# Last level of a triangular inverse on compact blocks of two matrices, in a two-block transformer kernel

## The reference, cut to what matters

```python
    A = jnp.where(strict, jnp.einsum('bhntk,bhnsk->bhnts', kb, k) * Lmat, 0.0)
    eye = jnp.eye(C, dtype=A.dtype)
    T = lax.linalg.triangular_solve(eye + A, jnp.broadcast_to(eye, A.shape),
                                    left_side=True, lower=True, unit_diagonal=True)
    u = jnp.matmul(T, v * beta[..., None])
    w = jnp.matmul(T, kb * jnp.exp(gam)[..., None])
```

## Time and profile before

| what | value |
|---|---|
| median of 3 runs | 1431.57 us (1431.5 to 1432.8) |
| the profiled execution | 1431.52 us |
| its span, first to last instruction | 1429.8 us |
| TensorE, matmul / weight load | 98% / 93% busy |
| VectorE / ScalarE | 68% / 56% busy |
| mean granted TensorE clock | 0.999 |

### The profile page before, as it was taken

One profiled execution on the slowest core, in us unless ns is written; L12 is line 12 of the kernel. 1 busy time (PEld: TensorE's weight loads), 2 busy tenths in 40 slices (PEclk: granted clock), 3 DMA queues, 4 the chain that ended last, 5 costly groups with the idle time before them and its releaser, 6 DMA issues.

```text
span 1429.8 us, 28104 instructions
## 1 busy us (share of the span) xinstructions
PE 1405.7 (98%) x10598; PEld 1330.5 (93%) x10598; DVE 969.4 (68%) x1441; ACT 799.5 (56%) x1289; POOL 28.7 (2%) x73
## 2 busy tenths in 40 slices
PE   8999999999999999999999999999999999999998
PEld 8999999979999889999899999999999899899997
DVE  5786677676455575555688888888888755654554
ACT  4345444644444454444568788788788743544443
POOL 6000000000000000000000000000000000000000
PEclk9999999999999999999999999999999999999999
DMA  8465555555555645665574444534543356566651
GB/s 257 145 178 147 140 131 156 192 177 177 191 191 176 207 146 177 182 193 183 143 182 119 127 108 117 144 99 112 144 115 119 90 149 206 159 189 186 196 183 59
DMA packets 304641, 224.94 MB, mean 157 GB/s; under 512 B 10419, under 2 KB 288069, under 8 KB 304581
## 3 DMA queue, kind: packets, MB, share of 16 engines
q1 hardware_dynamic: 304580, 224.09, 53.1%
HBM read 223.02 MB, written 1.05 MB: 157 GB/s over the span
## 4 chain that ended last, share of the span: by engine, by line
PE 91%; DVE 4%; ACT 2%; DVEq 1%; issue 1%; POOL 0%; ACTq 0%; POOLq 0%
PE G L1758 19%; PE G L1760 19%; PE G L1759 19%; PE M L1763 5%; PE M L1764 5%; PE M L1765 5%; PE M L1758 2%; PE M L1760 2%; PE M L1759 2%; PE M L2230 1%; DVE w_lo L1045 1%; PE M L2243 1%; PE M L2213 1%; PE M L2202 1%; ACT w_hi L573 1%; DVEq L1042 1%
## 5 line engine op out<-in xcount | busy, mean ns | idle before, releaser
L1758 PE MATMUL G<-xa_hi,w_hi 128*128 128x256 f32 x2152 | 629.4, 292 | 2.0 <-DVE w_lo L1045 1.4
L1045 DVE TENSOR_TENSOR w_lo<-w_raw,w_hi 128x2048 fp32r<-128x2048 f32 (+1 forms) x208 | 475.2, 2286 | 228.7 <-ACT w_hi L573 224.1
L1760 PE MATMUL G<-xa_hi,w_lo 128*128 128x256 f32 x2152 | 608.6, 283 | 0.0
L1759 PE MATMUL G<-xa_lo,w_hi 128*128 128x256 f32 x2152 | 608.2, 283 | 0.0
L573 ACT ACTIVATE w_hi<-w_raw 128x2048 fp32r<-128x2048 f32 x207 | 394.6, 1908 | 236.3 <-PE G L1760 134.2
L1758 PEld LDWEIGHTS G<-xa_hi,w_hi 128*128 128x128 f32 x2152 | 411.0, 191 | 9.4 <-issue 7.1
L1759 PEld LDWEIGHTS G<-xa_lo,w_hi 128*128 128x128 f32 x2152 | 411.2, 191 | 2.8 <-issue 1.7
L1760 PEld LDWEIGHTS G<-xa_hi,w_lo 128*128 128x128 f32 x2152 | 410.5, 191 | 0.1
L1763 PE MATMUL M<-w_hi,xb_hi 128*128 128x512 f32 x304 | 118.9, 391 | 0.9 <-DVE xb_lo L1045 0.7
L1764 PE MATMUL M<-w_lo,xb_hi 128*128 128x512 f32 x304 | 118.7, 390 | 0.0
L1765 PE MATMUL M<-w_hi,xb_lo 128*128 128x512 f32 x304 | 118.3, 389 | 0.0
(11 more groups left out here) (357 smaller groups left out, 2029.3 us busy)
## 6 DMA issues: line engine op xcount, KB each, us to landing
w_raw<-in_w_in SPq DMA_DIRECT2D x166, 512.0 KB, 4.7
w_raw<-in_ffn_w_in SPq DMA_DIRECT2D x88, 512.0 KB, 5.0
w_raw<-in_w_ff SPq DMA_DIRECT2D x64, 512.0 KB, 4.1
w_raw<-in_ffn_w_out SPq DMA_DIRECT2D x44, 512.0 KB, 3.7
w_raw<-in_w_out SPq DMA_DIRECT2D x16, 512.0 KB, 4.2
w_raw<-in_w_branch_gdn SPq DMA_DIRECT2D x16, 512.0 KB, 5.1
w_raw<-in_w_branch SPq DMA_DIRECT2D x12, 512.0 KB, 4.3
w_raw<-in_w_branch_hgrn SPq DMA_DIRECT2D x8, 512.0 KB, 4.0
```

Of the source, the lines that this page charges most:

```text
L1045: return v.tensor_tensor(dst, src, hi.bitcast(F32), ALU.subtract)
L1758: mm(out_, w[0], x[0], start=first, stop=False)
L1759: mm(out_, w[0], x[1], start=False, stop=False)
L1760: return mm(out_, w[1], x[0], start=False, stop=last_)
```

## The change

The last level, too, works on compact blocks. z(6) is two matmul calls with n21 as weights, a new tile that holds the right halves of both matrices of nt; ScalarE fills it at the end of the head before. z_copy(6) and inv_t(5) take the form of the lower levels, so there is a compact(5) on ScalarE. w(6) comes out turned, two calls of 64 columns. yi is then put together from its parts: ScalarE's new `y_diagonal` copies the four diagonal quarters from bank 5 (four instructions of 64 partitions), y_copy(5) copies only the lower right blocks into yc, and VectorE copies w into the off-diagonal quarters with two copies. The tile xc gets space of its own.

In the queues: on ScalarE level_exp(8) moves ahead of the split, and split_j(1) moves behind compact(5) and z_copy(6), ahead of y_copy(5). In the last head ScalarE's split and VectorE's w_low of a later chunk move behind y_diagonal and behind scored(8).

```diff
-    xc = grid(yi.rearrange("p i e c -> p (i e c)")[:, 2 * P:4 * P], i=TT, e=2, c=HD)
+    xc, n21 = (grid(mix(2 * P), i=TT, e=2, c=HD) for _ in range(2))
...
                 act.wait_ge(zz_done, l + (i - 1) * 6)
-                if l == LEVELS - 1:
-                    nc.scalar.activation(halved(zi.rearrange("p i e c -> p (i e c)"), l, 0), packed(M[:, 3, 0:T], l),
-                                         ACT.Copy).then_inc(zc_ready, 1)
-                    return
...
                 else:
-                    nc.scalar.activation(yi.rearrange("p i e c -> p (i e c)"), M[:, 5, :], ACT.Copy).then_inc(yy_ready, 1)
+                    nc.scalar.activation(yc[:, :, HD:P], M[:, 5, 0:T].rearrange("p (i c) -> p i c", i=TT)[:, :, HD:P],
+                                         ACT.Copy).then_inc(yy_ready, 1)
+
+            def y_diagonal():
+                if not main:
+                    return
+                for side in range(2):
+                    half = slice(HD * side, HD * side + HD)
+                    for e in range(2):
+                        ins = nc.scalar.activation(yi[half, :, e, half], M[HD * e:HD * e + HD, 5, 0:T].rearrange(
+                            "p (i c) -> p i c", i=TT)[:, :, half], ACT.Copy)
+                ins.then_inc(yy_ready, 1)
...
             if main:
                 level_exp(7)
-            if gemm:
-                split_j(1)
-            else:
+                level_exp(8)
+            compact(5)
+            z_copy(6)
+            split_j(1)
+            y_copy(5)
+            y_diagonal()
+            if not gemm:
                 act_split(c0 + 5 + RING - 6)
-            if main:
-                level_exp(8)
-            z_copy(6)
-            y_copy(5)
...
                 level_exp(2, i + 1)
+                nc.scalar.activation(n21, nt[:, :, :, HD:P], ACT.Copy)
...
-        v.memset(zi, 0.0)
...
                     dve.wait_ge(wt_done, i)
-                    dve.sem_inc(waited, 1)
-                    v.copy_predicated(halved4(yi, l, 1), halved(lmask[:, l, :].bitcast(I32), l, 1).unsqueeze(1).to_broadcast(shape),
-                                      packed(M[:, 5, 0:T], l).rearrange("p (x n) s -> p x n s", x=4)).then_inc(yy_ready, 1)
+                    for e in range(2):
+                        ins = v.tensor_copy(yi[0:HD, :, e, HD:P],
+                                            M[HD * e:HD * e + HD, 4, 0:P].rearrange("p (i c) -> p i c", i=TT))
+                    ins.then_inc(yy_ready, 1)
...
             decayed(7)
-            if not gemm:
-                w_low(c0 + 5 + RING - 6, i, 6)
             decayed(8)
...
             scored(8)
+            if not gemm:
+                w_low(c0 + 5 + RING - 6, i, 6)
...
                 if l == LEVELS - 1:
-                    four(3, nt, xi, l, 0, zz_done)
+                    for b in range(TT):
+                        ins = mm(M[:, 3, P * b:P * b + P].rearrange("p (e c) -> p e c", e=2), n21[:, b, :, :].rearrange("p e c -> p (e c)"),
+                                 xi[:, b, :, 0:HD], start=True, stop=True)
+                    ins.then_inc(zz_done, 1)
                     return
...
                 if l == LEVELS - 1:
-                    four(5, zi, yi, l, 1, wt_done)
+                    for b in range(TT):
+                        ins = mm(M[:, 4, HD * b:HD * b + HD], zd[:, b, :, :].rearrange("p e c -> p (e c)"), yc[:, b, HD:P],
+                                 start=True, stop=True)
+                    ins.then_inc(wt_done, 1)
                     return
...
-                if l < LEVELS - 2:
-                    pe.wait_ge(xc_ready, l + 1 + (i - 1) * 5)
-                    for b in range(TT):
-                        ins = nc.tensor.transpose(M[:, 5, P * b:P * b + P], xc[:, b, :, :].rearrange("p e c -> p (e c)"), ident[:])
-                    ins.then_inc(yt_done, 1)
-                    return
-                pe.wait_ge(xx_ready, l + (i - 1) * 5)
+                pe.wait_ge(xc_ready, l + 1 + (i - 1) * 6)
                 for b in range(TT):
-                    for e in range(2):
-                        at = T * b + P * e
-                        ins = nc.tensor.transpose(M[:, 5, at:at + P], xi[:, b, e, :], ident[:])
+                    ins = nc.tensor.transpose(M[:, 5, P * b:P * b + P], xc[:, b, :, :].rearrange("p e c -> p (e c)"), ident[:])
                 ins.then_inc(yt_done, 1)
```

More of the change, by code:

```diff
@@ L2207, in level @@
                 ins.then_inc(lev_done, 1)
-            def four(out_bank, lhs, rhs, l, side, done):
-                for b in range(TT):
-                    for e in range(2):
[L2212 to L2215, removed]
             def inv_z(l):
@@ L2237, in inv_w @@
                 pe.wait_ge(zc_ready, l + (i - 1) * 6)
-                pe.wait_ge(yy_ready, l + (i - 1) * 7)
+                pe.wait_ge(yy_ready, l + (i - 1) * 8)
                 if l == LEVELS - 1:
-                    four(5, zi, yi, l, 1, wt_done)
+                    for b in range(TT):
+                        ins = mm(M[:, 4, HD * b:HD * b + HD], zd[:, b, :, :].rearrange("p e c -> p (e c)"), yc[:, b, HD:P],
+                                 start=True, stop=True)
+                    ins.then_inc(wt_done, 1)
                     return
@@ L2282, in head @@
             if main:
-                pe.wait_ge(yy_ready, i * 7)
+                pe.wait_ge(yy_ready, i * 8)
                 for e in range(2):
```

## The result

The changed kernel takes 1438.50 us (median of six runs, 1438.12 to 1439.73), the kernel before 1432.16 us (six runs taken with it, 1431.5 to 1432.8). The ratio is 1.0046, with a 95% interval of [1.0034, 1.0059]: slower by 6.3 us, where 5.3 had been forecast.

What follows compares the result with a forecast made beforehand. TensorE, busy 98%, was taken as the bound, with VectorE having no slack at the border of two heads. 1431.5 + 3.5 (loop) + 1.8 (last head) = 1436.8 us; range 1431.5 to 1440.8 us.

Steps and rivals of the forecast that it cites:

- The loop's term: Borders between heads: each next head begins 0.5 us late, 7 borders x 0.5 = +3.5 us.
- VectorE's slack: VectorE behind ScalarE's late exponential: idle times of 0.45 and 0.37 us cut 1.26 us of lateness to about 0.5.
- TensorE's savings: Last level on TensorE: z(6), turns and w(6) save 1.12 us per head, 9.0 in eight, if nothing waits.
- Rival 4: New w(6) passes get no cheaper, staying at 0.84 us; time about the forecast; chance 0.6 together with the forecast.
- ScalarE's order: Loop head: split ahead of y_copy(5) makes w(6) wait 1.14 us; with y_diagonal's 1.14, table load 1.64 us late.
- rival 1: y_diagonal's small copies overlap on ScalarE, 0.60 us in all; sum +1.9, 1433.4 us; chance 0.18.
- The last head: Last head: split behind y_diagonal makes the table load 2.40 us late and the turn of hrs late: +1.8 us.
- the named chain: Last head: late split, table load 2.40 us late, scaling at L893 2.11 late, then the turn of hrs: +1.8 us.
- The other named wait: Last head: cross product (L2304) waits for w_low, begins near 1143.85 us; the later wait for L893 swallows it.
- Rival 2: TensorE's savings arrive at w(6) of the loop's heads, 1.12 us per head; 1422.5 us with all eight; chance 0.13.
- Rival 3: y_diagonal takes 1.28 us: +6.5; with a narrow wait opening every head, 2.8 more: 1440.8 us; chance 0.09.
- narrow waits: gsq_ready and y0_ready, next late in the queues, stay narrowly in time; one opening would cost 0.4 us per head.

Runs made afterwards that it cites:

- run 1: Changed kernel with split_j(1) moved behind y_copy(5) and y_diagonal in the loop: 1442.02 us, ratio 1.0069.
- run 3: Changed kernel with three of y_diagonal's four quarter copies left out: 1434.00 us, ratio 1.0017.
- run 4: Kernel before with five unread 64x128 ScalarE copies added behind y_copy(5) in the loop's heads: 1436.02 us, ratio 1.0031.
- run 11: Changed kernel without VectorE's subtraction for the low part of the delta layer's output in the loop's heads: 1434.04 us, ratio 1.0019.
- Run 12: Changed kernel with the edits of run 2 and run 5, and without the subtraction that run 11 leaves out: 1426.99 us, ratio 0.9968.
- run 9: Changed kernel with the edits of run 2 and run 5, and the xb_lo subtraction moved from VectorE to GpSimd: 1433.09 us, ratio 1.0010.
- run 10: Kernel before with the xb_lo subtraction moved from VectorE to GpSimd, nothing else: 1431.32 us, ratio 0.9999.
- run 5: Changed kernel with the last head's split and w_low put back where they stood before: 1438.39 us, ratio 1.0041.
- run 7: Kernel before with inverse(1) ahead of scored(0) on VectorE: 1431.65 us, ratio 0.9997.
- run 2: Changed kernel with split_j(1) back ahead of level_exp(8) and compact(5) in the loop: 1432.37 us, ratio 1.0007.
- run 6: Changed kernel with inverse(1) ahead of scored(0) on VectorE, TensorE's wait for the scored block adapted: 1438.70 us, ratio 1.0047.
- run 8: Changed kernel with the edits of run 2, run 5 and run 6 together: 1431.54 us, ratio 0.9998.

## Why the prediction was right, and by how much it was off

**Direction and mechanism.** Right. The 1.1 us that leave TensorE in each head were given back at w(6), and the head's length followed from ScalarE's later table load by way of VectorE (runs 1, 3, 4 and 11). The sum came 1.0 us too low by the medians. The loop's term was 1.3 us too low, 0.8 of it because VectorE's slack was taken too large.

**TensorE's savings.** 0.47, 0.18 and 0.47 were forecast for z(6), the turns and w(6). z(6) gave 0.44, since the old one took 0.81 and not w(6)'s 0.84, and the turns 0.23. The new w(6) takes 0.44 and not 0.37, so its saving is 0.40; it starts behind a wait, and the stalled w of the earlier trace rows was 0.07 longer too. Sum 1.07 for 1.12. Rival 4, passes no cheaper than before, is out.

**ScalarE's order.** w(6) begins at 775.61 (forecast 775.53). The 1.11 us of the profile are not the forecast's 1.14, though they look alike: the forecast counted from the time at which TensorE could have begun, 774.39, and by that count it is 1.2. Next matmul at 776.05 (775.97); y_diagonal 1.11 (1.14), at the lower end neither 0.60 nor at 1.28: the four quarter copies don't overlap, so rival 1 is out, and the two of them that cross partitions are no longer than the rest (0.26 to 0.27 us each); table load at 776.49 (776.56). From the split's start to y_copy it was 1.94 and not 1.80, made up by a z_copy 0.04 earlier and a y_copy that lets y_diagonal begin after 0.17 in place of 0.31. n21 ends at 802.55, within the stretch in which ScalarE waits 1.50 for z(1): covered, as said.

**VectorE's slack: the term that was mis-sized.** L1630 came 1.30 late (1.26), L1636 0.94 (0.8), L1691 0.64 (0.5), and the head 0.69 longer (0.5). I had subtracted the idle times 0.45 and 0.37 of the earlier trace rows nearly whole, with 0.05 kept back for both. But 1.30 - 0.94 = 0.36 was absorbed where 0.45 was idle, and 0.94 - 0.64 = 0.30 where 0.37 was. The missing 0.07 to 0.09 is still there in the changed kernel, where neither instruction waits for anything: L1636 begins 0.07 behind the end of the one before it, L1691 0.08. That part of an idle time isn't slack. Another 0.04 came from L1630 and 0.04 from a head that started earlier. The loop's term is 7 x 0.69 = 4.8 and not 3.5 us. Lateness is absorbed here in pieces, and the small remainder is what is paid seven times, so the 0.11 us that the two pieces were taken too large cost 0.8 us in the sum.

**The last head.** +1.8 forecast, +1.76 measured, by the named chain: the split, the table load, L900, the turn. The other named wait, for w_low before the cross product, is there as well (1.07 before L2302) and, as said, the later wait of 1.22 covers it.

**Rival 2** (the savings arrive) had 13% of the chance. Run 12 shows the part of it that is true: 0.47 us per head of the matmuls come through once the split is back and VectorE has 0.6 less to do. In the kernel as changed none did. The Trainium skill (Perfetto Trace Analysis, "Identifying the Most-Contended Engine") says to optimize the engine with the highest occupancy first. That engine is TensorE here, at 98%, and of the work that the change takes off it nothing came through. The busy shares of the whole span, 98% and 68%, don't show how close VectorE stands in the loop. The kernel before, its seven loop heads (window, length, busy times of PE, PEld, DVE, ACT and POOL, clock, DMA):

```profile
740.00:1118.00 378.00, 377.74 (x3158) 372.71 (x3158) 326.75 (x692) 305.54 (x699) 0.00 (x0) 1.00 0.46 122
```

VectorE is busy for 86% here, and once ScalarE is late it has no wait on another engine from evac[1] to inverse(2) of the next head.

**Rival 3.** Neither of its narrow waits (y0_ready, gsq_ready) opened in the changed kernel. The one before y0 opened in run 9.

## What to carry to other kernels

Two engines that meet once per turn of a loop share its length: work taken off the busier one counts only as far as the other can follow, so follow each edit from the engine it touches to the point where they meet, and add the work it puts on a third engine that feeds them. A new wait of a microsecond on the busiest engine is a symptom first; move it (run 1) and lighten what stands behind it (run 3) before blaming it. When idle times are used up as slack, try how far two such instructions stand apart when neither waits (0.07 to 0.08 us here), and leave that much of each.

## What the runs showed that was not expected

**GpSimd beside VectorE's scans.** A subtraction of 128x512 on GpSimd, 1.17 us long, stretched a pair of 128x128 scans on VectorE that ran beside it from 0.73 to 1.59 us (run 9). It is the second scan alone that is longer, 1.25 for 0.40 us, and it ends 0.28 behind GpSimd's end (850.04 and 849.76). Why was not tried; that it costs VectorE more than the operation itself would (0.86 for 0.60) is shown; the scans are as long in all seven heads of runs 9 and 10.

**TensorE's clock behind an idle stretch.** In the profiled run TensorE stood idle for 1.55 us before z(2) of head 8, having waited 0.48 a few us earlier. In the kernel before the same place has 1.36 and 0.48. The timeline of the changed kernel:

```profile
1127.19 0.97 PE L2233 MATMUL M<-arena 128*128 128x128 f32 x4 [1.55 <-DVE arena L1543]
...
1128.81 1.91 PE L2169 MATMUL G<-masks,ident 128*128 128x256 f32 x4
...
1131.38 1.03 PE L2169 MATMUL G<-masks,ident 128*128 128x256 f32 x4
```

and its windows (window, length, then busy times of PE, PEld, DVE, ACT and POOL, granted clock, share and rate of the DMA):

```profile
1127.00:1131.00 4.00, 3.81 (x15) 3.45 (x16) 1.75 (x6) 3.38 (x11) 0.00 (x0) 0.57 0.76 212
1131.00:1135.00 4.00, 3.93 (x26) 3.21 (x26) 3.12 (x7) 2.54 (x7) 0.00 (x0) 1.00 0.00 0
```

The same four matmuls take 1.91 us at 0.57 of the clock, near its lower level of 1.2 GHz, and 1.03 at the full 2.4 GHz. The profiled run of the kernel before, of the lower group, keeps 1.00 from 1115 to 1165 us. At 0.57 for 4 us the changed kernel lost 0.43 x 4 = 1.7 us of clock, about the 1.6 by which the spans differ beyond the 6.6 worked out above. The other traces fit. Of the fourteen profiled runs seven are of their kernel's upper group (the changed kernel, runs 1, 3, 5, 7, 10 and 11), and each has such a dip, 0.57 or 0.58 over 4 us: five at the start of head 8 and two, runs 7 and 11, near 512 us. The seven of the lower groups have none before their last microseconds. The dips begin near the end of a longer idle time of TensorE, 1.3 to 1.6 us in head 8, 1.93 and 1.90 at 511. The idle time alone doesn't decide it, for the kernel before has the same 1.93 there and keeps 1.00 from 508 to 516 us. For the runs that were not profiled only the mean clock is known; it is lower in the upper groups, 0.997 or 0.998 with a few at 0.999.

**Idle time at the start of a turn of the loop.** z(1) began behind 0.25 to 0.41 us of idle time marked issue in six heads of the changed kernel (2.0 us in the waits), against 0.19 to 0.24 in run 4 and 0.17 once in run 2. In run 11, where VectorE is lighter, it is gone. The timelines show what goes with it. The last matmuls in front of z(1) are two turns (L2371) that need VectorE's copy out of G (L1709); the changed kernel at the first border:

```profile
802.18 0.41 DVE L1709 COPY arena<-G 128x256 f32<-128x256 f32 x1
802.68 0.41 PE L2371 MATMUL M<-ident,arena 128*128 128x128 f32 x2
803.39 0.61 PE L2233 MATMUL M<-arena 128*128 128x128 f32 x4 [0.30 <-issue]
```

Where the turns begin less than 0.1 us behind the end of that copy (the changed kernel, runs 1, 4, 5 and 6), z(1) follows their start by 0.60 to 0.84 us. With 0.15 to 0.19 (runs 2 and 8) it is 0.47 to 0.73, with 0.43 to 0.50 (the kernel before, runs 3, 7, 9 and 10) 0.22 to 0.46, and with 0.68 or more (runs 11 and 12) 0.21 or 0.22. So this idle time comes with a late VectorE, and it is a second place where the two engines meet at the border; what the queue does in it is open.

**A quarter costs half of the whole.** A copy of 64x128 from PSUM on ScalarE takes 0.28 us, whether it keeps its partitions (z_copy, 0.56 for two) or not (y_diagonal, 1.11 for four, two of which cross from one half of the partitions to the other), and one copy of all four quarters took 0.60.
